# A hybrid diffusion step: state-space mixer laid out feature-major, exponents made in PSUM, gate moved under the output projection

## Reference

```
q, k, v, z, xbc, dt = split(h @ w_in)
na  = neighbourhood_attention(q, k, v)              # 8 heads of 64
xbc = silu(dwconv3(xbc)); x, B, C = split(xbc)      # x: 16 heads of 64; B, C: 2 groups of 128
dt  = softplus(dt + dt_bias); A = -exp(a_log)       # one per direction and head
# for both directions, chunk by chunk of 128 tokens, state h of (128, 64) per head:
cum = cumsum(dt * A)
y   = (C B^T * exp(cum_i - cum_j) * dt_j, masked to j <= i) @ x  +  (C @ h) * exp(cum)
h   = h * exp(cum_last) + B^T @ (exp(cum_last - cum) * dt * x)
y   = y_fwd + y_bwd + d_skip * x
y   = rmsnorm(y * silu(z)) * norm_g
x0 += gate * (concat(na, y) @ w_out);  x0 += gate * (relu(norm(x0) @ w1)^2 @ w2)
```

## Time and profile before

| | us |
|---|---|
| runs | 3556.30, 3557.57, 3557.73 |
| median | 3557.57 |
| the profiled execution | 3556.85 |
| its span, first to last instruction | 3555.0 |
| attention, with z | 309 to 541 |
| convolution | 541 to 786 |
| preparation | 786 to 801 |
| scan | 801 to 1032 |
| gate | 1033 to 1079 |
| output projection of layer 0 | 1079 to 1236 |

### The profile page before, as it was taken

The page is one execution under the profiler, slowest core; times in us unless marked ns, Lnnn a source line. Parts: engine busy times, 40 slices in busy tenths (PEclk is TensorE's granted clock), DMA queues, the critical chain, the costliest instruction groups (busy, mean ns, idle before and its releaser), DMA issues. The chain is left out here.

```text
span 3555.0 us, 46469 instructions
## 1 busy us (share of the span) xinstructions
PE 3324.5 (94%) x18040; PEld 2879.2 (81%) x18040; DVE 2001.8 (56%) x3367; ACT 911.5 (26%) x1743; POOL 593.4 (17%) x550
## 2 busy tenths in 40 slices
PE   7999998978959999999999979999988999999997
PEld 5665554544539999999999968888888999999996
DVE  4995541247974755544555577565456554455446
ACT  2213441122133431121112153322243122111221
POOL 1010000017641310111101002322232011111110
PEclk6999999999979999999999999999999999999998
DMA  5661001000024311111111022222142111111111
GB/s 234 235 266 44 24 22 51 24 0 24 1 116 114 115 42 42 36 47 41 43 42 39 24 93 62 60 66 64 51 131 83 42 36 47 41 41 35 47 47 54
DMA packets 161694, 233.52 MB, mean 66 GB/s; under 512 B 17260, under 2 KB 135700, under 8 KB 156812
## 3 DMA queue, kind: packets, MB, share of 16 engines
q1 hardware_dynamic: 161548, 231.53, 19.4%
HBM read 214.86 MB, written 16.63 MB: 65 GB/s over the span
## 5 line engine op out<-in xcount | busy, mean ns | idle before, releaser
L1639 PE MATMUL PS<-AHL,WH 128*128 128x384 f32 x3072 | 782.8, 335 | 6.0 <-DVE WL L1907 6.0
L1639 PE MATMUL PS<-Y,WH 128*128 128x384 f32 x3072 | 780.1, 334 | 3.1 <-issue 3.1
L1927 DVE SCALAR_TENSOR_TENSOR XT<-PS,MOD,XT 128x384 f32<-128x384 f32 (+2 forms) x1024 | 495.0, 514 | 225.2 <-PE PS L1639 225.1
L1639 PEld LDWEIGHTS PS<-AHL,WH 128*128 128x128 f32 x3072 | 557.5, 189 | 6.6 <-DVE WL L1907 6.6
L1639 PEld LDWEIGHTS PS<-Y,WH 128*128 128x128 f32 x3072 | 554.5, 188 | 4.2 <-issue 3.7
L1639 PE MATMUL PS<-AHL,WL 128*128 128x384 f32 x1536 | 514.9, 335 | 0.0
L1639 PE MATMUL PS<-Y,WL 128*128 128x384 f32 x1536 | 513.0, 334 | 0.0
L1914 DVE TENSOR_TENSOR AHL<-SQ,AHL 128x384 fp32r<-128x384 f32 x192 | 157.4, 820 | 433.0 <-ACT AHL L1740 433.0
L1841 POOL TENSOR_TENSOR SQ<-RT 128x384 f32<-128x384 f32 x192 | 180.2, 938 | 1319.2 <-ACT RT L1735 1299.8
L602 PE MATMUL PS<-HT,WR 128*128 128x384 f32 x960 | 323.2, 497 | 18.2 <-DMA WR<-in_wslots 10.9
L1729 ACT ACTIVATE WH<-WU 128x1024 fp32r<-128x1024 f32 x128 | 135.5, 1059 | 726.8 <-DMA WU<-in_wff 726.8
(11 more groups left out here) (331 smaller groups left out, 4443.4 us busy)
## 6 DMA issues: line engine op xcount, KB each, us to landing
WU<-in_wff SPq DMA_DIRECT2D x128, 512.0 KB, 3.5
XT<-in_wmod SPq DMA_DIRECT2D x13, 2048.0 KB, 10.1
F<-in_wmod SPq DMA_DIRECT2D x9, 2048.0 KB, 9.1
OWR<-in_wslots SPq DMA_DIRECT2D x24, 768.0 KB, 5.0
WR<-in_wslots SPq DMA_DIRECT2D x8, 2048.0 KB, 8.2
PW<-in_wslots SPq DMA_DIRECT2D x24, 512.0 KB, 4.6
OWOR<-in_wslots SPq DMA_DIRECT2D x24, 512.0 KB, 4.2
EX<-b_rows SPq DMA_DIRECT2D x72, 128.0 KB, 3.2
```

Of the source, the lines that this page charges most:

```text
L1639: mm = nc.tensor.matmul(out, wt(w), x, start=(n == 0 and i == 0), stop=(n == len(terms) - 1 and i == 2))
L1927: ins = nc.vector.scalar_tensor_tensor(out=x, in0=PS[:, 3 + j % 4, a - c * TC:e - c * TC], scalar=MOD[:, l, 40 + b, cond:cond + 1], in1=x, ...
```

## The change

- **z** is made feature-major: weights as stationary operand, 384 tokens as moving one, 24 tiles of 8 products, put into the attention's steps by sixteenths (`gate_pieces`: 5 or 6 products a step, three ahead of the turn). It is stored by block of features, and so is the attention's output (`yna_spill`, nine DMAs). One weight slot of the convolution is loaded two thirds into the attention.
- **Convolution**: the four blocks of B and C come first; a block is turned in thirds, the first two behind the second and third tile of the next block and the last behind the first tile of the one after. The preparation is spread over these blocks (`prep` on each engine). The skip term is made by ScalarE with a column of d (`DX`) and stored to DRAM (`skip_spill`). The running sums of the decays are also made as rows, split into a high and a rest part, and stored (`cum_rows`, `cum_parts`).
- **Scan**: y is kept feature-major in three chunks (`YL`). The exponents are made in PSUM by two fp32r products per bank of four heads: identity times mask, and ones times the two split rows, loaded by DMA; ScalarE takes the exponential of each head alone (16 of 128x128) with a bias from `NB` = ln(dt) - cum, so that dt is in it and `xdt` is gone. The state read is 8 products of 128x128 by 128 columns; the chunk's output is 16 products whose stationary operand is 128x64, for even heads into partitions 0 to 63 and for odd ones into 64 to 127, summed over both directions in PSUM, opened and closed by products of zeros. exp(cum) for the read state comes from DRAM rows spread over partitions (`EB`, two DMAs of 256 KB a step in 512 B pieces) and one exponential of 128x1024. The state's decay moves from VectorE to GpSimd (`carry`).
- **Gate**: the stage is gone. Chunk 0 is gated at the start of `out_and_mlp`, chunks 1 and 2 under the products of the chunk before; the mean square comes from products with ones (`gate_sum`: 8, 4 and 4). x is loaded again in thirds (`x_again`) in that stage.

```
@@ out_and_mlp, SP
+                        gate_in(0)
+                        for n in range(3):
+                            out_weights(sp, kk, n)
+                        x_again(0)
+                        gate_in(1)
+                        x_again(1)
+                        x_again(2)
+                        gate_in(2)
@@ out_and_mlp, TensorE
+                    def gate_sum(c):
+                        if c == 0:
+                            for b in range(KD):
+                                pe.wait_ge(square_sum_ready.sem, b // 4 + 1)
+                                mm = nc.tensor.matmul(PS[:, 0, 0:TC], ones, ZH[0][:, b, :], start=(b == 0), stop=(b == KD - 1))
@@ scan, TensorE
+                def exponents(n, b):
+                    j = 4 * n + b
+                    if j >= 2:
+                        pe.wait_ge(exp_ready.sem, exp_ready.at(4 * (j - 1)))
...
+                    nc.tensor.matmul(PS[:, 2 + j % 2, :].rearrange("p (h i) -> p h i", h=4), ident_r[:, :],
+                                     mask_r[:, n % 2, :].unsqueeze(1).broadcast_to((P, 4, P)), start=True, stop=False)
+                    nc.tensor.matmul(PS[:, 2 + j % 2, :], ones_r[r, :], CR[r, 512 * b:512 * b + 512], start=False, stop=True)\
+                      .then_inc(exponents_made.sem, 1)
...
+                for n in range(NS):
+                    more = n + 2 < NS
+                    if n + 1 < NS:
+                        read(n + 1)
+                    if more:
+                        exponents(n + 2, 0)
+                    if n + 1 < NS:
+                        update(n + 1)
+                    if more:
+                        exponents(n + 2, 1)
+                    chunk(n, 0)
+                    if more:
+                        exponents(n + 2, 2)
+                    chunk(n, 1)
+                    if more:
+                        exponents(n + 2, 3)
@@ scan, VectorE
+                for n in range(NS):
+                    if n + 1 < NS:
+                        inter(n + 1)
+                    if n % 2 == 0 and n >= 2:
+                        output(n // 2 - 1, n + 2 if n + 1 < NS else NS)
+                    if n + 1 < NS:
+                        weights(n + 1)
+                        add_state(n + 1)
@@ scan, GpSimd (before: RW 128x2048, xdt and xw per step)
+                for n in range(NS):
+                    if n + 1 < NS:
+                        carry(n + 1)
+                    if n + 2 < NS:
+                        inputs(n + 2)
@@ convolution, TensorE
+                    for c in range(NC):
+                        feature_tile(pe, i * NC + c, slot_k(S_XBC + i // 4), (i % 4) * P, c, banks=4)
+                        b = i - 2 if c == 0 else i - 1
+                        if b in turns:
+                            turn(b, (c - 1) % NC)
+                    prep(i)
@@ attention, TensorE
-                    for q in range(4 * n, 4 * n + 2):
-                        gate_product(pe, q, S_Z, (6, 7))
+                    for q in gate_pieces(n)[:3]:
+                        gate_product(pe, q, (6, 7))
```

1163 lines of the change are left out of this document (717 added, 446 removed).

## The result

| | us |
|---|---|
| before, five runs | 3548.36 to 3560.12, median 3557.57 |
| after, five runs | 3524.27, 3527.21, 3534.45, 3536.44, 3540.04, median 3534.45 |
| ratio | 0.9941, 95% interval 0.9929 to 0.9954 |
| predicted | 3475, range 3440 to 3518 |
| profiled execution of after | 3524.27, span 3522.5 |

The change makes the kernel 0.6% faster: a gain of 23 us where 82 were forecast. The profiled execution is the fastest of the five, so the pair of profiles shows more than the medians: 32.5 us by their spans.

A forecast was written before the change was run, and what follows sets the result against it. TensorE was taken as the bound, except in the scan, bound by VectorE slowed by GpSimd. Gains of 16 (to the scan), 54 (scan) and 12.5 (gate), 82.5 off 3556.85, gave 3474.4 profiled, median 3475 us, range 3440 to 3518.

The forecast's parts named there:

- another 2.5 for a cold start: Convolution: 2.5 us for the cold start, beside 3 us for remaining waits, within a forecast 229 us.
- exponents 8 fp32r products of 512 columns ... 0.236 each, 1.9: Scan, TensorE: eight exponent products at 0.236 us each, 1.9 us a step, scaled by columns from a 384-column product's 0.177.
- hardly over VectorE's: Scan bound: exponents at float32 pace take 3.4 us, making TensorE's step 9.4 or 9.5, barely above VectorE's 9.2.
- VectorE's 9.2: Scan: VectorE sets the step at 9.2 us, gaps included, with bounds 6.9 and 10.7.
- 177: Scan: 177 us in all against 231.5 before, a gain of 54 with bounds 76 and 29.
- 16.7 + 4: Scan outside its 17 steps: 16.7 us before they run and 4 for the last chunk and output.
- The order in TensorE's queue costs nothing: Scan: update, three exponents, chunk and read, 7.9 us behind VectorE's state update, fit into VectorE's 9.2, so no cost.
- hidden: Scan: rows and pairs, asked for two to three steps ahead, take 2 us of transfer a step and cost nothing.
- Rival 3: Scan: TensorE's clock falls to half through short waits, scan 293 us, whole 3591; 5 in 100.
- Rival 4: Scan: a wait in a ring of queues makes the step 12 to 14 us, no engine full, whole 3540; 7 in 100.
- 3 us; clock 1.5: Gate under projection: later stalls cost 3 us and the clock 1.5, within a forecast gain of 12.5.
- about 1 us late: Gate under projection: GpSimd's last rests for tiles 8 and 16 come about 1 us late, part of the 3 us stalls.

The follow-up runs named there:

- e1: The kernel after the change with each 512-column exponent product made as two of 256; median 3572.32 us, ratio 1.0050 to the kernel before.
- e2: The kernel after the change with each 512-column exponent product made as one of 384 and one of 128; median 3575.17 us, ratio 1.0074 to before.
- e5: The kernel after the change with its zero products made with all 128 rows instead of one; median 3504.61 us, ratio 0.9872 to before.
- e6: The kernel after the change with the 128-row mask product repeated in place of the two-row product, result incomplete; median 3513.13 us, ratio 0.9886 to before.
- e3: The kernel after the change without the zero products that open and close y's banks; median 3503.98 us, ratio 0.9856 to before.
- e4: The kernel after the change with VectorE's output ahead of the next step's decay of the read; median 3498.30 us, ratio 0.9841 to before.
- e7: The kernel after the change with the scan's first transfers asked for in another order; median 3529.40 us, ratio 0.9936 to before.
- e9: The kernel after the change with the edits of e3, e4 and e8 together; median 3479.30 us, ratio 0.9792 to before.
- e11: The kernel after the change with gate arithmetic of chunks 1 and 2 on 8 of 384 columns, result incomplete; median 3520.69 us, ratio 0.9905 to before.
- e13: As e11, with GpSimd's rests of chunks 1 and 2 also cut to 8 columns and left out of the result; median 3509.45 us, ratio 0.9874 to before.
- e8: The kernel after the change with the next chunk's gate sum, mean, root, scalings and rests one output tile sooner; median 3531.29 us, ratio 0.9948 to before.
- e10: The kernel after the change with the edits of e4, e5 and e8 together; median 3496.05 us, ratio 0.9841 to before.
- e12: e9 with ScalarE's four first parts of a tile moved behind the norm's steps; median 3482.08 us, ratio 0.9804 to before.

## Why the prediction was wrong

**Attention and the convolution's start: right.** First product 545.21 for 545, TensorE's first wait now behind the queue of the stage and not for weights:

```profile
545.21 2.23 PE L624 MATMUL PS<-HT,WR 128*128 128x384 f32 x3 [4.64 <-PEq L869]
```

**Convolution: right mechanism, term too small.** Its last tile ended at 764.7, forecast 774. TensorE is busy 219.49 of 219.70 us. The waits for the Silu went wholly, where I had kept 3 us and another 2.5 for a cold start, and the work itself was 3 to 4 us less than the 215 and 8 I had added up. The tail of 11.3 us (764.7 to 776.0) had been put at 11 to 12. One reading was off by little: by columns a z product of 512 costs 0.87 and not 0.86, so z was 125.2 us before as well as now. Gain 25 instead of 16. This was read from the two traces and not tried by an experiment.

**Scan: the step that failed is "exponents 8 fp32r products of 512 columns ... 0.236 each, 1.9".** The price was scaled by columns from products in a row of equal ones. By columns it was right; but here every fp32r product stands between neighbours of another shape and pays 0.10 us at each side: 0.427, and 3.4 us a step (e1, e2, e5, e6). The 3.4 stood in the prediction as a bound, for another reason, and with "hardly over VectorE's". The zeros pay the same, 0.75 for 0.5. TensorE's step is 9.75 us of work, not 8.0, and it is the bound (e3: work taken away shows one for one). By itself this would have cost little, since VectorE's 9.2 had been taken as the step: 0.55 us in 17 steps, 9 of the 40 us by which the scan missed 177. The rest are terms that the sum had at nothing: 16 us of TensorE's idle time (0.93 a step), 13 that the steps hold beyond work and idle time and that go with the clock, and 2 outside the steps (22.6 for 16.7 + 4).

The idle time is two things. One is the order of the queues, by the prediction's step "The order in TensorE's queue costs nothing". VectorE's output stands behind the decay of the read, and TensorE waited 11.3 us for it in the profile, 8.6 of that within the steps; with the output ahead of the decay e4's scan came out 18 us shorter. The other is 6.7 us for the rows of step 2, where the prediction has rows and pairs as "hidden"; e7 shows that another order of the transfers takes most of this wait away.

The clock had a rival of its own and no term. TensorE's work a step divided by the granted clock gives 9.75 / 0.90 = 10.8 for after, 9.75 / 0.83 = 11.7 for e7, 9.0 / 0.90 = 10.0 for e3, 9.75 / 0.93 = 10.5 for e4, 9.55 / 0.97 = 9.8 for e5, 9.0 / 0.97 = 9.3 for e9; with the idle time of the table this comes out 0.2 to 0.5 us above each of their measured steps. (For e1 and e2 it gives more than was measured, since at the lower level a product of theirs took 0.51, not twice 0.31.) What the step holds beyond work and idle time is 0.8 us in the profile of after and 1.1 to 1.7 in the other four with its steps, so 13 to 29 us in all go with the lower clock. Counted by stretches it is the same: the profile of after has four falls of 6.8 us behind its first steps, those of e11 and e13 have six, and those of e7 and e8 seven. Each follows a wait for VectorE's output, and without these waits (e4, e9, e10, e12) there is none; so in this kernel most of the clock's cost came by the order of the queues too. It also explains why the medians differ by 23 us where the profiled pair has 32.5: the other profiles of these steps have lower clocks and scans of 224 to 230 us.

VectorE's side was sound: the weights took 1.67 us in the mean, with GpSimd's work halved, and VectorE was left idle. It was not far from being the bound, though: in e9, where TensorE was busy all the time from 830 to 920 us, VectorE was busy 84.4 of these 90, about 8.4 us of a step of 8.96, where 9.2 had been forecast. Rival 3 (the clock falls) was right in kind, with its short waits as what goes ahead of a fall, and wrong in size: the level changed for parts of the scan and not for all of it. Rival 4 (a ring of queues, 3540) has nearly the measured time by luck: of its mechanism only the output's wait is there, and TensorE, which it has as not full, is the bound.

**Gate under the projection: start right, end wrong.** Tile 0 was ready at 32.8 us (forecast 34). The step that failed is "3 us; clock 1.5" for the later waits: they are 25. The tally had VectorE's excess per tile but took GpSimd's rests as "about 1 us late". Their work is half of it (e13), and neither an earlier place (e8) nor another order (e12) helps. At tile 8 the rests themselves are slow: the last three took 5.99 us, where three of 1.06 are 3.2. At tile 16 they are late because they stand behind the norm's sum of squares, at the end of a chain through ScalarE's square and VectorE's addition; VectorE was busy 24.6 of 28.4 us there, with rounds of 10.7 us a tile (1126.17 to 1136.90) where 8 to 8.5 had been forecast. That it is this chain which makes up tile 16's wait is read from the traces of after, e11 and e13; no run takes the sum of squares away.

## What to carry to other kernels

A price per column is good only among equal neighbours. When a product uses another part of the array than those beside it, add the price of the change at both sides, and then fewer and fuller products win: 128 rows of zeros cost less than one row, and splitting made it worse. When the bound is to move to another engine, write out that engine's new step with its order and clock before counting the gain; after that, look for what stands in a queue ahead of the one result that it waits for. Here such a wait cost twice, once by itself and once by the clock behind it. Work moved under another stage's products is free only if each helper engine, GpSimd too, fits into every tile.

## What the runs showed of the hardware

- An fp32r product of 512 columns took 0.23 us among equals, 0.33 with one neighbour of another shape and 0.43 with two. Shapes here are 1 or 2 rows by 128, 128 by 128, and 128 by 64.
- 512, 384, 256 and 128 columns between unlike neighbours: 0.427, 0.37, 0.31 and 0.26 us.
- TensorE's clock went to the lower level in stretches of the scan in which it was busy all the time. Behind the scan's first steps (from about 820 us) the order was this. With waits of 1.2 to 1.8 us for VectorE's output every other step and zero products of one row, or none (after, e3, e6, e7, e8, e11, e13), every fall within the steps came 1.5 to 2.8 us after the end of such a wait (one in e6 during a wait of 3.7 us), though not every wait had one. With the same waits and zero products of 128 rows (e5) there was no fall. Without the waits (e4, e9, e10, e12) there was none either. With twice as many exponent products and no such wait (e1, e2) the clock was 0.77 and 0.75 from 838 us to the scan's end. So neither the wait nor the thin products alone orders these runs; what exactly sets the level is open.
- VectorE and GpSimd together: GpSimd's rest of 128x384 took 1.06 us before and 1.47 in the mean in the new stage.
